# Sparse attention's front in a two-block transformer kernel: raw key and value rows projected once, queries ahead of the compression, other keys and values between its steps

## The reference

```python
kv = (xs @ w_kv).reshape(B, S, 3, 2, G, hd)          # 3 branches x (key, value) x 4 groups x 64
pieces = kv[0] in strides of 16;  blocks = two neighbouring pieces (32 tokens) + cmp_pe
hid  = gelu(einsum('cbgnf,cfh->cbgnh', flat(blocks), cmp_w1) + cmp_b1)   # 15 blocks, 32*64 -> 256
comp = einsum('cbgnh,chd->cbgnd', hid, cmp_w2)       # compressed keys and values
slc = kv[1];  win = kv[2]                            # selected and window keys and values
q = (h @ w_in)[..., :1024] * hd**-0.5;  gate = sigmoid((h @ w_in)[..., 1024:])   # 16 heads, 3 gates each
p_cmp = masked_softmax(q . k_cmp);  out = gate0*o_cmp + gate1*o_slc + gate2*o_win
```

## Time and profile before

| what | us |
|---|---|
| median of three runs | 3227.07 (3219.3 to 3228.28) |
| the profiled execution | 3225.99 |
| its span in the trace | 3223.9 |
| TensorE busy | 2971.4 (92%) |
| VectorE busy | 2083.7 (65%) |
| ScalarE busy | 1487.0 (46%) |
| granted TensorE clock, mean | 0.957 |

### The profile page before, as it was taken

The page is one execution under the profiler, slowest core; times in us unless marked ns, Lnnn a source line. Parts: engine busy times, 40 slices in busy tenths (PEclk is TensorE's granted clock), DMA queues, the critical chain, the costliest instruction groups (busy, mean ns, idle before and its releaser), DMA issues.

```text
span 3223.9 us, 54246 instructions
## 1 busy us (share of the span) xinstructions
PE 2971.4 (92%) x18082; PEld 2637.8 (82%) x18082; DVE 2083.7 (65%) x3950; ACT 1487.0 (46%) x2826; POOL 60.5 (2%) x118
## 2 busy tenths in 40 slices
PE   5898999989999789999999999888889999999998
PEld 4678878778889579999988888765689999988886
DVE  3325895458965658888976666224268888966665
ACT  0103454234543234447975555103244448965554
POOL 0000110001100000000000000000000000000000
PEclk9899999999999899999999999986899999999999
DMA  5135984459954244554245665450145553256563
GB/s 165 56 103 172 303 321 118 131 153 347 347 170 143 79 137 162 182 182 137 99 141 191 193 194 165 135 116 1 27 150 182 182 180 113 98 170 193 192 194 118
DMA packets 318588, 519.29 MB, mean 161 GB/s; under 512 B 40865, under 2 KB 219425, under 8 KB 317858
## 3 DMA queue, kind: packets, MB, share of 16 engines
q1 hardware_dynamic: 302082, 457.83, 45.0%
q0 software_dynamic: 16416, 60.30, 5.1%
HBM read 517.02 MB, written 1.05 MB: 161 GB/s over the span
## 4 chain that ended last, share of the span: by engine, by line
PE 82%; ACT 7%; DVE 5%; issue 3%; DMA 2%; ACTq 1%; SPq 0%; DVEq 0%
PE ps L880 29%; PE ps L808 10%; PE ps L812 10%; PE ps L809 10%; PE ps L783 3%; PE ps L742 2%; PE ps L857 2%; DMA tile_ring<-mlp_w_in 2%; ACT spread L1681 1%; PE ps L753 1%; ACT spread L1687 1%; PE ps L766 1%; ACT hot_pair L1681 1%; PE ps L1336 1%; PE ps L1288 1%
## 5 line engine op out<-in xcount | busy, mean ns | idle before, releaser
L808 PE MATMUL ps<-x_high,w_high 128*128 128x256 f32 x3200 | 799.4, 287 | 44.7 <-ACT w_high L1490 25.7
L809 PE MATMUL ps<-x_low,w_high 128*128 128x256 f32 x3200 | 790.7, 284 | 0.0
L808 PEld LDWEIGHTS ps<-x_high,w_high 128*128 128x128 f32 x3200 | 618.4, 193 | 50.3 <-ACT w_high L1490 28.3
L1832 DVE TENSOR_TENSOR w_low<-tile_ring,w_high 128x512 fp32r<-128x512 f32 x688 | 472.2, 693 | 271.1 <-ACT w_high L1530 179.9
L809 PEld LDWEIGHTS ps<-x_low,w_high 128*128 128x128 f32 x3200 | 619.0, 193 | 0.1
L812 PE MATMUL ps<-x_high,w_low 128*128 128x256 f32 x3200 | 450.8, 284 | 0.0
L880 PE MATMUL ps<-w_high,x_high 128*128 128x512 f32 x1376 | 426.9, 392 | 19.9 <-DVE x_low L1827 19.9
L880 PE MATMUL ps<-w_high,x_low 128*128 128x512 f32 x1376 | 425.9, 391 | 0.0
L880 PE MATMUL ps<-w_low,x_high 128*128 128x512 f32 x1376 | 425.8, 391 | 0.0
L1661 ACT ACTIVATE w_high<-tile_ring 128x1024 fp32r<-128x1024 f32 x256 | 269.8, 1055 | 314.6 <-PE ps L812 314.2
L812 PEld LDWEIGHTS ps<-x_high,w_low 128*128 128x128 f32 x3200 | 414.8, 193 | 0.0
(11 more groups left out here) (321 smaller groups left out, 3270.8 us busy)
## 6 DMA issues: line engine op xcount, KB each, us to landing
tile_ring<-peer_u SPq DMA_DIRECT2D x256, 512.0 KB, 3.2
tile_ring<-peer_v SPq DMA_DIRECT2D x256, 512.0 KB, 4.3
arena<-mod_w POOLq DMA_DIRECT2D x112, 512.0 KB, 6.5
tile_ring<-mlp_w_in SPq DMA_DIRECT2D x64, 512.0 KB, 5.5
tile_ring<-mlp_w_out SPq DMA_DIRECT2D x64, 512.0 KB, 6.5
tile_ring<-ret_w_in SPq DMA_DIRECT2D x48, 512.0 KB, 3.9
tile_ring<-peer_w_q SPq DMA_DIRECT2D x32, 512.0 KB, 4.0
tile_ring<-sb_w_qkv SPq DMA_DIRECT2D x24, 512.0 KB, 4.5
```

The source lines that it names most:

```text
L808: nc.tensor.matmul(dst, cols, x_high[:, c, :], start=c == 0, stop=False)
L809: nc.tensor.matmul(dst, cols, x_low[:, c, :], start=False, stop=False)
L1832: return V.tensor_tensor(w_low[:, k % 2, cols], tile_ring[:, k, cols], w_high[:, k % 2, cols].bitcast(F32), ALU.subtract)
```

## The change

The four raw units become two plain units (one panel of 256 columns each, for key and for value). Their results are lifted to the even places of `raw`, and TensorE makes the places with exchanged halves from them: for each half one product of 64 columns of the identity with 512 columns of `raw`. The four query units and the gate unit are moved ahead of the compression, the first query unit ahead of the exchange; their input goes to `hot_rows` instead of `xn`, right after the layer norm. The selected keys and values are made behind the compression's products, ahead of its transposes; the window's behind the scores, ahead of the transposes of the picks. SyncE's refills, VectorE's lifts and ScalarE's sigmoid are put in the same order. The clearing of `pick` comes after the gate's lift. The unit count stays at 20 for the two stages together.

```diff
-                        ("weigh0", T // 4), ("shared", 11), ("nsa", 9), ("route1", 18), ("weigh1", T // 4)):
+                        ("weigh0", T // 4), ("nsa", 20), ("route1", 18), ("weigh1", T // 4)):
@@ SyncE
-            panels(4, issue_raw, by_unit())
-            units.up(4)
-            panels(4, lambda i, s: issue_kv(i + 2, s), by_unit())
-            units.up(4)
-            sp.wait_ge(unit_done, units.n - 7)
-            sp.dma_start(b1_row, I["cmp_b1_2"].unsqueeze(0)).then_inc(b1_loaded, 16)
...
-            panels(4, issue_w1, by_use())
-            bare.up(4)
-            units.up(3)
...
-            panels(4, issue_q, by_unit())
-            units.up(4)
...
+            panels(2, issue_kv, by_unit())
+            units.up(2)
+            panels(1, issue_q, by_unit())
+            units.up(1 + 2)
+            panels(3, lambda i, s: issue_q(i + 1, s), by_unit())
+            units.up(3)
             panels(1, issue_gate, by_unit())
-            units.up(1 + 4)
+            units.up(1)
+            sp.wait_ge(unit_done, UNITS["nsa"] + 1)
+            sp.dma_start(b1_row, I["cmp_b1_2"].unsqueeze(0)).then_inc(b1_loaded, 16)
+            panels(4, issue_w1, by_use())
+            bare.up(4)
+            panels(2, lambda i, s: issue_kv(i + 2, s), by_unit())
+            units.up(2 + 3 + 2)
+            panels(2, lambda i, s: issue_kv(i + 4, s), by_unit())
+            units.up(2 + 2)
@@ TensorE
             pe.wait_ge(modulated, norms.n * C)
+            stream(2, feature_major(xn))
+            wait_operand()
+
+            def query(i):
+                s = slot_ready(4)
+                u = open_unit()
+                w = ring[:, s, :].rearrange("p (c r m) -> p c r m", r=2, m=P)
+                for r in range(2):
+                    for c in range(C):
+                        mm = nc.tensor.matmul(ps[:, u % BANKS, r * T:(r + 1) * T], w[:, c, r, :], hot_rows[:, c, :],
+                                              start=c == 0, stop=c == C - 1)
+                mm.then_inc(unit_done, 1)
+            query(0)
             for c in range(2):
-                for pair in range(2):
...
-            for body in (feature_major(xn), token_major(xn), feature_major(xn), token_major(xn)):
-                stream(1, body)
+                pe.wait_ge(unit_taken, UNITS["nsa"] + c + 1)
+                u = open_unit()
+                for odd in range(2):
+                    mm = nc.tensor.matmul(ps[odd * NSA_D:(odd + 1) * NSA_D, u % BANKS, :],
+                                          ident[:, (1 - odd) * NSA_D:(2 - odd) * NSA_D], raw[:, c, 0:NSA_G:2, :],
+                                          start=True, stop=True)
+                mm.then_inc(unit_done, 1)
+            for i in range(1, 4):
+                query(i)
+            stream(1, token_major(hot_rows, 48))
             wait_operand()
@@ after the compression's products
+            stream(1, feature_major(xn))
+            stream(1, token_major(xn))
             pe.wait_ge(cmp_ready, 2)
@@ the queries' old place
-            wait_operand()
-            for i in range(4):
...
-            stream(1, token_major(xn, 48))
             all_taken()
@@ ScalarE
+            act.wait_ge(unit_taken, UNITS["nsa"] + 9)
+            A(gate, gate, ACT.Sigmoid).then_inc(silu_ready, 1)
             for c in range(2):
                 act.wait_ge(panel_used, ROWS["compression"] + 2 * (c + 1))
...
-            act.wait_ge(unit_taken, UNITS["nsa"] + 5)
-            A(gate, gate, ACT.Sigmoid).then_inc(silu_ready, 1)
@@ VectorE
-            for c in range(2):
-                take(2, lambda i, u: V.tensor_copy(raw[:, c, 2 * i:2 * i + 2, :], bank2(u)))
-            for kT, vt in ((kT_slc, v_slc), (kT_win, v_win)):
-                take(1, lambda i, u: V.tensor_copy(kT, bank2(u)))
-                take(1, lambda i, u: V.tensor_copy(vt, bank2(u)))
+            operand(modulate(48, hot_rows))
+            take(2, lambda i, u: V.tensor_copy(raw[:, i, 0:NSA_G:2, :], bank2(u)))
+
+            def lift_query(first):
+                return lambda i, u: V.tensor_scalar(QT[:, 2 * (first + i):2 * (first + i) + 2, :], bank2(u), float(NSA_D ** -0.5),
+                                                    None, ALU.mult)
+            take(1, lift_query(0))
+            take(2, lambda i, u: V.tensor_copy(raw[:, i, 1:NSA_G:2, :], bank2(u)))
...
             operand(ins)
+            take(3, lift_query(1))
+            take(1, lambda i, u: V.tensor_copy(gate, bank2(u, 48)))
             bare.up(4)
+            V.memset(pick, 0.0).then_inc(pick_cleared, 1)
+
+            def lift_keys(kT, vt):
+                take(1, lambda i, u: V.tensor_copy(kT, bank2(u)))
+                take(1, lambda i, u: V.tensor_copy(vt, bank2(u)))
+            lift_keys(kT_slc, v_slc)
             take(1, lambda i, u: V.tensor_copy(cmp_hid, bank(u)[:, 0:4 * NSA_G * N_CMP].rearrange("p (c f n) -> p c f n", c=2, f=2)))
...
-            V.memset(pick, 0.0).then_inc(pick_cleared, 1)
             v.wait_ge(pick_cleared, 1)
-            operand(modulate(48))
-            take(4, scaled_pair(QT, float(NSA_D ** -0.5)))
-            take(1, lambda i, u: V.tensor_copy(gate, bank2(u, 48)))
...
             V.tensor_tensor(slot, slot, pick_sum.unsqueeze(3).broadcast_to(wide), ALU.mult).then_inc(pick_weighed, 1)
+            lift_keys(kT_win, v_win)
             take(2, copy_pair(pickT))
```

More of the change, by code:

```diff
@@ L1280, in _ @@
             pe.wait_ge(modulated, norms.n * C)
-            for c in range(2):
-                for pair in range(2):
[L1283 to L1290, removed]
-            for body in (feature_major(xn), token_major(xn), feature_major(xn), token_major(xn)):
-                stream(1, body)
+            stream(2, feature_major(xn))
[10 more added lines that the diff above has]
+            query(0)
+            for c in range(2):
+                pe.wait_ge(unit_taken, UNITS["nsa"] + c + 1)
[8 more added lines that the diff above has]
+            stream(1, token_major(hot_rows, 48))
             wait_operand()
```

## The result

The changed kernel took 3178.36 us in the median of four runs (3174.83 to 3183.02), the kernel before 3227.47 (four runs, 3219.30 to 3228.28): a ratio of 0.9854, interval 0.9842 to 0.9866. The profiled execution took 3174.83 us, against 3225.99: 51.2 less. Two stretches hold all of it. The front, from the end of the eighth `xn` chunk to the first attention score, went from 149.1 to 114.4. The attention, from its first score to the first zero product of the output projection, went from 107.7 (2183.4 to 2291.1) to 90.2 (2149.4 to 2239.6). The two make 52.2, the spans differ by 50.7: the rest is 1.5 us the other way.

What follows compares the result with a forecast made beforehand. The prediction took TensorE, busy 92% of the span, as the bound. Its terms, savings less added costs, summed to -35.3 us (35.6 by the path check), giving 3191.5 us, range 3182 to 3202.

Steps and rivals of the forecast that it cites:

- tail: Short steps between the selected units and the first score product, transposes to last lift: 4.7 us in place of 8.75.
- entry: Last term of the forecast path, up to the first attention score: 1.8 us, with pick transposes 0.9 us shorter.
- stall of 10.8: TensorE's wait ahead of the compression while VectorE makes the 32 block sums; the moved queries would hide all 10.8 us.
- slow start of 2.4: The compression's first half running at a low clock after the wait for the block sums; 2.4 us would go.
- the one of 4.9: TensorE's wait before the transposes of the picks, during the small softmax; window units would cover it, -4.9 us.
- drain at each change of width: Around the identity products, changing tiling mode might drain TensorE: at most 0.46 us for each of four changes, 1.9 us.
- sums exposed: Rival: TensorE still waits for the compression's block sums, so 10.8 and 2.4 us come back: 3204.7 us, chance 0.03.
- the ring becomes the bound: Rival: panel loads arrive too slowly for the units; 3238 us if a panel took 18 us; chance 0.03.
- the clock holds through the tail: Rival: full clock lasts into the scores (-3.7 us) and window units start fast (-3.1): 3184.7 us, chance 0.14.
- the clock is worse: Rival: narrow gate unit counts as idle, attention entry gains nothing, identity products run singly: 3197.8 us, chance 0.20.
- step 7: Attention entered behind dense work at full clock: pick transposes -0.9 us, from the first scores -1.5, bounds 0 and -5.
- bound of 24 us: If the attention lost all its full-clock share, its busy part would double, up to 24 us: 3216, held unlikely.

Runs made afterwards that it cites:

- e8: Kernel before with only the first part: raw rows in two plain units and the exchange by identity products, order otherwise as before; 3211.51 us, ratio 0.9959.
- e1: Changed kernel with the two window units moved back ahead of the compression's transposes, right behind the selected ones; 3194.85 us, ratio 0.9903.
- e10: Changed kernel with eight useless transposes ahead of each of the attention's 14 waits for a score bank; 3165.60 us, ratio 0.9820.
- e11: Changed kernel with one useless full product ahead of each of the attention's 14 waits for a score bank; 3178.91 us, ratio 0.9861.
- e5: Changed kernel with two useless full products ahead of each of the attention's 14 waits for a score bank; 3169.48 us, ratio 0.9827.
- e12: Changed kernel with four useless full products ahead of each of the attention's 14 waits for a score bank; 3175.55 us, ratio 0.9851.
- e15: The changed kernel run once more, unaltered; 3177.24 us, ratio 0.9852.
- e9: Changed kernel with the window's keys made before the scores and two useless full products ahead of each attention wait; 3162.03 us, ratio 0.9810.
- e3: Changed kernel with five VectorE memsets before the lifts of the picks, so TensorE idles ahead of the attention; 3199.65 us, ratio 0.9914.
- e2: Kernel before with 32 useless full products between the scores and the transposes of the picks; 3225.45 us, ratio 1.0002.
- e4: Changed kernel with 8 more useless full products (3.5 us) ahead of the transposes of the picks; 3190.69 us, ratio 0.9890.
- e7: Changed kernel with the window's keys made before the scores, its values still behind them; 3176.66 us, ratio 0.9849.
- e6: Kernel before with two useless full products ahead of each of the attention's 14 waits for a score bank; 3207.00 us, ratio 0.9942.
- e13: Kernel before with eight useless transposes ahead of each of the attention's waits for a score bank; 3204.29 us, ratio 0.9927.

## Why the prediction was wrong

**What was right: the front.** Its path was forecast at 114.9 and measured 114.4. By its steps: plain units 16.9 (16.5), exchange 2.0 (1.87), q1 to q3 20.7 (20.9), gate 3.5 (3.5), compression 15.3 (15.2), selected units 13.8 (14.0), tail 4.7 (4.5), scores 12.4 (13.0), window units with a slow start 16.9 (16.0), entry 1.8 (1.9); the first query unit took its 6.9. The steps missed by up to 0.9 us, and their misses nearly cancel. The stall of 10.8 and the slow start of 2.4 went to nothing behind the queries, the one of 4.9 behind the window units. The identity products did run side by side, at the lower bound: 1.87 us for eight records is 0.23 each, half of L903's 0.46 in the earlier trace rows. The drain at each change of width, which the Trainium skill names (TensorEngine Tiling (Array Packing), section "Key Properties"), was priced at 1.9 us more; neither the changed kernel's trace nor e8's shows anything like it. The rivals "sums exposed" and "the ring becomes the bound" did not occur, "the clock holds through the tail" neither: the scores ran at 0.50.

That the front came out within 0.5 us is in part luck. The first term of the rival "the clock is worse", a slow start of the compression behind the narrow gate unit, did not occur in this execution, but it did in e1, e10 and e11, at 3.3 us and not 2.4. Among the six profiled executions that share the changed kernel's front (changed, e5, e10, e11, e12, e15) the front took from 113.0 to 118.3 us. The working also has a slip: 3190.7 and 1.1 make 3191.8; the 3191.5 belongs to the path's 35.6.

**What failed: step 7, the attention's entry.** I gave it "-1.5 (...; bounds 0 and -5, since most of what follows waits on softmax chains)" in the attention; it was -17.5 in the profiled execution. The miss is the whole of the error: without it the profiled execution would have come out at 3191. So the price of the attention's clock is the term that was mis-sized. Three things were wrong in that step.
- The reason. TensorE was busy 92.3 of 107.2 us, 15.6 of the first 16.4. That is a stage bound by TensorE at the lower level, and I read it as one bound by chains. The chains bound it only once the clock is up: with the level held, 83.5 to 85.4 us in e5, e9 and e10, so 22 to 24 us were there to be had. My own bound of 24 us for losing the clock's full share shows that I had the size in hand, on one side only.
- The duration. I assumed that the upper level would last a few microseconds past the dense work. In the changed kernel it lasted through the first 16 us entirely.
- The range. It took "some us" of the attention's clock either way. The runs put the four attentions entered low at 103.2 to 107.7 us (before, e1, e3, e8) and the four entered high at 90.2 to 99.8 (changed, e2, e4, e7).

From these eight, entry is worth 8.6 us on the mean (105.4 against 96.8). The other part of the 17.5 is how long the upper level lasts after a high entry: 90.2 twice in the changed kernel, 97.3 in e2, 99.8 in e4 and e7. That is not settled. A shift of the attention by 3.5 us of dense work (e4) moved it by 9.6 us. Nor is it settled why the attention's own start, 95% busy in the profile, stays at 0.50 for 16 us when two products or eight transposes in its waits bring it up. What moved the clock of the compression's first half in e1, e10 and e11, behind the same code, is as open.

## What to carry to other kernels

A stage in which TensorE is nearly always busy at 0.50 is bound by the clock, and its price must be worked out at both levels, because whatever is moved ahead of it can change which one it gets; here that was a third of the gain, and in e7 it ate a real one. Where a stage of short products and waits hovers between the levels, try useless products in the waits (two of 0.43 us were right here; one and four left the changed kernel's ratio of 0.9854 about where it was, at 0.9861 and 0.9851) before tuning its order, and judge other edits with the level held. For the rest, counting records at the two rates and placing waits behind moved units priced a front of 150 us to 0.5 us in one execution and to 4 us in others with the same front.

## What was not expected of the hardware

- Work that nobody needs made the kernel faster: 28 products, 12 us of TensorE at full clock, took 8.9 us off the changed kernel's median (3178.4 to 3169.5) and 18 off the kernel before (e6, 0.9942 with 0.9920 to 0.9964). In e5 the attention holds 4.9 of the 7.7 us between the profiled executions; the rest lies where the code is the same. In e6 it holds 18.0 of 22.7.
- Transposes did it as well as products, holding the level (e10, 0.98) and raising it (e13, 0.90).
- TensorE's clock stood at 0.69 over 11 us of the compression right behind the gate unit and with no wait between them, in 3 of 12 profiled executions of the new order (e1, e10, e11).
- Products of 512 columns that fill one half of the output partitions each run two at a time: 0.23 us a record against 0.46, with no pause at the change of width.
- The same attention, entered at the same level, took from 90.2 to 99.8 us depending on a few microseconds of dense work ahead of it.
